# Channel statistics of a convolution: eight 128-column sums against four 32-column strips with a folding product

## The chip, the cores and the metric

One core of a Trainium2 chip runs the whole program in one launch. The metric is the device time of that core in microseconds (us), median of the runs; lower is better.

## The reference, cut to what matters

The program is one inference step of a one-layer hybrid encoder on 320 tokens (256 prompt, 64 sample) with 1024 channels: input LayerNorm, one combined projection, a retention branch, a convolution branch, a gated merge of the two, and then a mixture of 32 experts. The change touches the LayerNorm inside the convolution branch and the gate that follows it:

```
c = lax.conv_general_dilated(u_pad, conv_w...)        # depthwise, width 31, 1024 channels
c = silu(layer_norm(c + conv_b, conv_ln_g, conv_ln_b)) # mean and variance over the 1024 channels
y_conv = c @ w_conv_out
a = (sigmoid(ga) * y_ret + sigmoid(gb) * y_conv) @ w_out
```

## The kernel before, in words

All activations between the input and the merge lie transposed: channels on the 128 partitions in KT = 8 tiles, tokens along the free axis. The convolution's result is `cT`, 128 x 8 x 350: 350 columns (CCOLS), of which 320 are tokens. Its mean over channels is therefore a sum over partitions and over 8 tiles, and TensorE makes it: `mean` (L1430 to L1439) multiplies a constant 128 x 128 matrix `meanw`, filled with 1/1024, with each tile of `cT` and accumulates the 8 products in bank 7 of PSUM, so that every partition of the bank holds the mean. The variance is made in the same way from the squares `sq` (L1445 to L1450). These products are fp32, and each shows in the trace as two MATMUL rows (two passes).

The weights of all dense products come as a stream of 45 chunks of 1 MB, in the order of the program: chunks 24 to 27 are the retention output (RET0), 28 to 31 the second gate (GB0 to GB0+3), 32 the embedding projection (PROJ0), 33 to 36 the convolution output (CONV0). For each chunk i, ScalarE makes a high part (`hi(i)`, L466) and VectorE the rest (`lo(i)`, L710), and TensorE forms three fp32r products of 320 columns for each of 8 x 2 weight tiles (`wide`, L1258 to L1268, products L1254 to L1256), 48 products in all. There are two buffers for the parts: `hi(i)` waits until TensorE has done chunk i-2, `wide(i)` waits for `lo(i)`.

The order on every engine is written out by hand. TensorE does: mean of tiles 0 to 4, chunk 28, mean of tiles 5 to 7, chunk 29, the eight products of `sq`, chunk 30, chunk 31, the projection in two column halves b = 0 and b = 1 (L1452 to L1474), chunk 33. VectorE and ScalarE each run a loop over i = 0 to 44 whose body begins with `lo(i)` or `hi(i)` and then does what is listed for that i:

- VectorE, i = 29: wait for the mean, subtract it from the 8 tiles (L1088). i = 30: the low part of the router weights and of `pT`, then wait for the variance, add EPS into `cstat` (L1096). i = 31: reciprocal (L1099), 8 products (L1101), low parts `CT_lo` (L1105). i = 32: more of these.
- ScalarE, i = 29: 8 squares (L607). i = 30: `pT_hi`. i = 31: square root of `cstat` (L589), then `silu` and high part (L599, L602) of tiles 0 and 1. i = 32: `silu` and high part of tiles 2 to 7.
- The sigmoid of a gate chunk (L595) stands in ScalarE's order by the table `SIGMOIDS_AT`: the chunks 28 and 29 one step after their number, 30 and 31 both at i = 33, behind `hi(33)` and all silus.

The projection's half b = 1 writes banks 7, 0 and 1, and waits for the sigmoid of chunk 30 to have read banks 0 and 1.

Of the kernel before, what the change touches and what calls it, by code (L numbers as in the profile page):

```python
# [9 lines left out]
TOK = SEQ + DEC_SEQ  # L10
TILES = 3
ROWS = [128, 128, 64]
KT = D_MODEL // 128
# [4 lines left out]
CCOLS = UCOLS - HIST  # L18
# [13 lines left out]
GLU0, QKV0, G0, GA0, RET0, GB0, PROJ0, CONV0, OUT0, GATE0, DENSE = 0, 8, 16, 20, 24, 28, 32, 33, 37, 41, 45  # L32
# [17 lines left out]
C_PRIO8 = C_PRIO4 + 4  # L50
C_FOLD = C_PRIO8 + 8
C_P = C_FOLD + 36
C_N = C_P + 1
NOWHERE = 4096

TAP_GROUPS = ((1, 2), (3, 4), (5, 6, 7))
# [4 lines left out]
def _constants():  # L61
    c = np.zeros((128, C_N), np.float64)
    p = np.arange(128)
    c[:, C_ID:C_ID + 128] = np.eye(128)
    c[:, C_ONES:C_ONES + 128] = 1.0 / D_MODEL
    scale = DK ** -0.5
    for h, g in enumerate(GAMMA):
        m = C_MASK + 448 * h
        for first, cols in ((0, np.arange(256)), (128, np.arange(128, 256))):
            src, dst = (first + p)[:, None], cols[None, :]  # L70
            seen = (dst >= src) | (dst // CHUNK == src // CHUNK)
            c[:, m + 2 * first:m + 2 * first + len(cols)] = np.where(seen, g ** np.abs(dst - src), 0.0) * scale
        l = np.arange(64)
        c[:64, m + 384:m + 448] = g ** np.abs(l[None, :] - l[:, None]) * scale
        c[:, C_XI + 64 * h:C_XI + 64 * (h + 1)] = g ** (l + 1.0)
        for t in range(TILES):
            last = 255 - 128 * t - p if t < 2 else np.maximum(63 - p, 0)
            c[:, C_ZETA + 4 * t + h] = g ** last * scale
    half = DK // 2
    inv = np.float32(10000.0) ** (-np.arange(half, dtype=np.float32) / np.float32(half))  # L80
    for t in range(TILES):
        pos = (128 * t + p if t < 2 else PAST_LEN + p % 64).astype(np.float32)
        ang = pos[:, None] * inv[None, :]
        c[:, C_COS + 64 * t:C_COS + 64 * (t + 1)] = np.cos(ang)
        c[:, C_SIN + 64 * t:C_SIN + 64 * (t + 1)] = np.sin(ang)
    c[:, C_IOTA:C_IOTA + 64] = np.arange(64)
    c[:, C_EOFF:C_EOFF + EXPERTS] = SLOTS * np.arange(EXPERTS)
    c[:, C_PRIO4:C_PRIO4 + 4] = 4 - np.arange(4)
    c[:, C_PRIO8:C_PRIO8 + 8] = 8 - np.arange(8)
    c[:72, C_FOLD:C_FOLD + 36] = np.concatenate([np.eye(36), np.eye(36)])  # L90
    c[:, C_P] = p
    return c.astype(np.float32)


# [25 lines left out]
def _program(nc, wstream, x, p_t, state_ret, state_conv, consts, triangle, conv_params, route_w, route_b,  # L120
             ln_in, ln1, ln2, y, ret_p, ret_s, conv_p, conv_s):
    F, R, B16 = mybir.dt.float32, mybir.dt.float32r, mybir.dt.bfloat16
# [17 lines left out]
    def area(name, size=None, skip=0):  # L140
        return Area(nc, spot[name] + skip, size if size else sizes[name] - skip)

    a = area("fixed")
    const = a.put("const", [128, C_N], F)
# [9 lines left out]
    a = area("split")  # L154
    whi = a.put("w_hi", [128, 2, CH], R)
    wlo = a.put("w_lo", [128, 2, CH], R)
    a = area("h")
    hT = [a.put("hT_hi", [128, KT, TOK], R), a.put("hT_lo", [128, KT, TOK], R)]
    uT = area("u").put("uT_sb", [128, KT, UCOLS], F)
    cT = area("c").put("cT_sb", [128, KT, CCOLS], F)  # L160
    a = area("qk")
# [3 lines left out]
    a = area("v")  # L165
# [8 lines left out]
    a = area("ret", end - spot["ret"])  # L174
# [7 lines left out]
    a = area("g")  # L182
# [7 lines left out]
    a = area("qk")  # L190
    AT = [a.put("AT_hi", [128, KT, TOK], R), a.put("AT_lo", [128, KT, TOK], R)]
    a = area("v")
    CT = [a.put("CT_hi", [128, KT, CCOLS], R), a.put("CT_lo", [128, KT, CCOLS], R)]
    sq = area("u").put("sq", [128, KT, CCOLS], F)
    a = area("h")
    mT = [a.put("m_hi", [128, KT, TOK], R), a.put("m_lo", [128, KT, TOK], R)]
    a = area("ret", end - spot["ret"])
    cstat = a.put("cstat", [128, CCOLS], F)
    at_tmp = Area(nc, spot["ret"] + 4096, 3584).put("at_tmp", [128, 2, TOK], F)

    a = area("h")
# [4 lines left out]
    a = Area(nc, spot["u"] + 2 * CH * 4, spot["v"] - spot["u"] - 2 * CH * 4)  # L206
# [5 lines left out]
    a = area("ga", end - spot["ga"])  # L212
# [5 lines left out]
    a = area("g", skip=CH * 4)  # L218
    logT = a.put("logT", [72, TOK], F)
    onehot = a.put("onehot", [128, TILES, SLOTS], B16, 2)  # L220
    a = area("fixed", 4 * (C_IOTA - C_MASK), skip=4 * C_MASK)
# [17 lines left out]
    a = Area(nc, pT_at, 7680)  # L239
# [22 lines left out]
        "affine_psum affine_T norm_ready h_rows hT_psum hraw_act hraw_dve hT_hi hT_lo ln_in_rows_in rows_scaled rows_done hT_last h1T_last gate_last hi_ready lo_ready pe_done wide_free row_free sig_ready v_ready qk_rows "  # L262
        "heads_T heads_copied kz_ready q_scaled scores masked kv_ready kv_out state_new o_ready on_ready "
        "diag_ready conv0_psum conv0_ready states_out ret_p_out out_tile route_hi route_lo "
        "onT_psum at_ready at_hi at_lo taps_done mean_ready centred squared var_ready cstd_ready conv_norm "
        "silu_ready ct_hi ct_lo m_ready m_hi_ready m_lo_ready out_evac "
        "var_in root_out h1_rows h1T_psum h1T_hi_s h1T_lo_s pT_hi_s pT_lo_s part_hi part_rest part_mid part_last "
        "logT_psum logT_ready logit_psum gexp_in gexp eexp_in eexp taken_ready rank_psum "
# [10 lines left out]
    def ss(name):  # L279
        return s[name]  # L280
# [177 lines left out]
    def _(act):  # L458
# [49 lines left out]
            go(kv_s[:], ps[:, 7, DV:2 * DV], ACT.Copy).then_inc(ss("kv_out"), 1)  # L508


        SIGMOIDS_AT = {c + 1: (c,) for c in [*range(GA0, RET0), GB0, GB0 + 1]}
        SIGMOIDS_AT[GB0 + 5] = (GB0 + 2, GB0 + 3)

        def merged_high(c):
            act.wait_ge(ss("m_ready"), c + 1)
# [186 lines left out]
    def _(dve):  # L702
# [338 lines left out]
        for i in range(DENSE):  # L1041
# [41 lines left out]
            conv(TAPS_AT.get(i, 0))  # L1083
            if i == 29:
                dve.wait_ge(ss("taps_done"), n_taps)
                dve.wait_ge(ss("mean_ready"), 1)
                for j in range(KT):
                    tt(cT[:, j, :], cT[:, j, :], ps[:, 7, 0:CCOLS], ALU.subtract).then_inc(ss("centred"), 1)  # L1088
            if i == 30:
                dve.wait_ge(ss("route_hi"), 1)  # L1090
                tt(w_route_r[:, :, 1, :], w_route[:], w_route_r[:, :, 0, :].bitcast(F), ALU.subtract).then_inc(ss("route_lo"), 1)
                dve.wait_ge(ss("pT_hi_s"), 1)
                tt(pT[1][:], pT_raw[:], pT[0][:].bitcast(F), ALU.subtract).then_inc(ss("pT_lo_s"), 1)
                dve.wait_ge(ss("var_ready"), 1)
                dve.wait_ge(ss("states_out"), 16)
                ts(cstat[:], ps[:, 7, 0:CCOLS], EPS, None, ALU.add).then_inc(ss("cstd_ready"), 1)  # L1096
            if i == 31:
                dve.wait_ge(ss("cstd_ready"), 2)
# [150 lines left out]
    def _(pe):  # L1249
# [5 lines left out]
            mm(out, wh, xl, start=False, stop=False)  # L1255
            return mm(out, wl, xh, start=False, stop=last)  # L1256

        def wide(c, par, src, cols, credit, banks=None):  # L1258

            pe.wait_ge(ss("lo_ready"), c)  # L1260
            pe.wait_ge(ss("wide_free"), credit)
            w = [q[:, par, :].rearrange("p (k c) -> p k c", k=KT) for q in (whi, wlo)]
            for t in range(2):
                out = ps[:, (2 * par if banks is None else banks) + t, 0:cols]
                for k in range(KT):
                    m = three(out, w[0][:, k, 128 * t:128 * t + 128], w[1][:, k, 128 * t:128 * t + 128],
                              src[0][:, k, :], src[1][:, k, :], k == 0, k == KT - 1)
            m.then_inc(ss("pe_done"), 1)  # L1268

        def last_tile(out_bank, x2, w, start, stop):  # L1270
# [161 lines left out]
        def mean(tiles):  # L1432
            for j in tiles:
                if j:
                    pe.wait_ge(ss("taps_done"), CONV_W * max(g[-1] for g in TAP_GROUPS if g[0] <= j))
                else:
                    pe.wait_ge(ss("conv0_ready"), 1)
                m = mm(ps[:, 7, 0:CCOLS], meanw, cT[:, j, :], start=j == 0, stop=j == KT - 1)
            return m  # L1439

        pe.wait_ge(ss("at_ready"), KT)
        mean(range(5))
        wide(GB0, 0, hT, TOK, 21)
        mean(range(5, KT)).then_inc(ss("mean_ready"), 1)
        wide(GB0 + 1, 1, hT, TOK, 22)  # L1445
        pe.wait_ge(ss("centred"), KT)
        for j in range(KT):
            pe.wait_ge(ss("squared"), j + 1)
            m = mm(ps[:, 7, 0:CCOLS], meanw, sq[:, j, :], start=j == 0, stop=j == KT - 1)
        m.then_inc(ss("var_ready"), 1)  # L1450
        wide(GB0 + 2, 0, hT, TOK, 23)
        wide(GB0 + 3, 1, hT, TOK, 24)  # L1452

        pe.wait_ge(ss("lo_ready"), PROJ0)
# [292 lines left out]
```

## Time and profile before

| what | value |
|---|---|
| median of 3 runs | 933.31 us (933.19 to 935.58) |
| the profiled execution | 933.24 us |
| its span in the profile | 931.1 us |
| TensorE busy | 867.5 us, 93% of the span |
| VectorE, ScalarE busy | 423.9 us, 260.0 us |
| chain that ended last | PE 56%, DMA 32%, DVE 6%, ACT 3% |

The profiled execution took 2.1 us more than its span, which begins with the first instruction and ends with the last. PE is TensorE (PEld its weight loads), DVE is VectorE, ACT is ScalarE, SP is the engine that issues the weight transfers. The statistics and the second gate lie between 267 and 316 us of the span. The experts' weights, 1 MB at a time, are streamed from 370 us to near 900 us.

### The profile page before, as it was taken

The page shows a single profiled execution, that of the slowest core. Times are in us where ns is not written, and L with a number is a line of the kernel's source. Part 1 is how long each engine was busy: PE and PEld are TensorE (multiplying, and loading weights), DVE is VectorE, ACT ScalarE, POOL GpSimd, SP SyncE. Part 2 cuts the span into 40 slices and gives each one's busy share as a digit, 9 for nine tenths or more (in the row PEclk, how much of TensorE's full clock was granted, in tenths as well). Part 3 has the DMA queues.
Part 4 walks back from the last instruction along what each step waited for, and adds up shares of the span by engine and source line. Part 5 has one row for each costly group of instructions (what it writes and reads, how often), then busy time and mean ns, then how long its engine had stood idle before and what let it go on. Part 6 is the DMA issues. An engine that isn't in the chain of part 4 may idle for free.

```text
span 931.1 us, 16368 instructions
## 1 busy us (share of the span) xinstructions
PE 867.5 (93%) x6542; PEld 558.8 (60%) x6542; DVE 423.9 (46%) x784; ACT 260.0 (28%) x356; POOL 49.4 (5%) x89
## 2 busy tenths in 40 slices
PE   8999999999999899899999999989888989898975
PEld 5997777789999796676444444434343434444431
DVE  6589799988967458965221111101010101011036
ACT  5451224444317723344112111111111212111110
POOL 1200000000000000000000000000000000000000
PEclk9999999999999999999999999999999999999997
DMA  8842233233433435945999999999999999999961
GB/s 318 274 164 72 99 146 118 91 113 114 150 139 133 147 136 180 372 152 223 414 420 421 422 422 421 422 422 421 423 422 423 422 422 421 422 422 422 421 253 56
DMA packets 40516, 266.66 MB, mean 286 GB/s; under 512 B 6214, under 2 KB 6486, under 8 KB 9632
## 3 DMA queue, kind: packets, MB, share of 16 engines
q1 hardware_dynamic: 36064, 255.30, 68.2%
q0 software_dynamic: 4416, 10.86, 3.6%
q8 instruction: 25, 0.41, 0.2%
q14 instruction: 11, 0.09, 0.0%
HBM read 258.38 MB, written 13.09 MB: 292 GB/s over the span
## 4 chain that ended last, share of the span: by engine, by line
PE 56%; DMA 32%; DVE 6%; ACT 3%; issue 2%; SPq 1%; DVEq 0%; ACTq 0%
DMA raw_x<-wstream 30%; PE ps L1557 12%; PE ps L1254 7%; PE ps L1255 6%; PE ps L1256 6%; PE ps L1568 3%; PE ps L1528 3%; PE ps L1291 2%; PE ps L1273 2%; PE ps L1292 2%; PE ps L1293 2%; PE ps L1351 2%; ACT w_hi L466 1%; DVE w_lo L710 1%; PE ps L1301 1%
## 5 line engine op out<-in xcount | busy, mean ns | idle before, releaser
L1557 PE MATMUL ps<-raw_x,xs 128*64 128x512 f32 x1024 | 233.6, 596 | 35.2 <-DMA raw_x<-wstream 34.0
L1557 PEld LDWEIGHTS ps<-raw_x,xs 128*64 128x64 f32 x1024 | 79.9, 136 | 160.3 <-issue 158.3
L710 DVE TENSOR_TENSOR w_lo<-raw_dense,w_hi 128x2048 fp32r<-128x2048 f32 x44 | 101.9, 2315 | 36.0 <-ACT w_hi L466 35.9
L1568 PE MATMUL ps<-raw_x,actT 128*64 128x512 f32 x512 | 117.8, 597 | 0.0
L1180 DVE COPY actT<-ps 128x256 f32<-128x256 f32 x32 | 13.6, 424 | 222.6 <-PE ps L1575 222.6
L466 ACT ACTIVATE w_hi<-raw_dense 128x2048 fp32r<-128x2048 f32 x44 | 84.0, 1908 | 97.7 <-PE ps L1273 62.7
L842 DVE SCALAR_TENSOR_TENSOR cT_sb<-uT_sb,conv_par,cT_sb 128x350 f32<-128x350 f32 x210 | 106.8, 574 | 0.6
L1254 PE MATMUL ps<-hT_hi,w_hi 128*128 128x320 f32 x304 | 95.5, 314 | 0.2 <-issue 0.2
L1256 PE MATMUL ps<-hT_hi,w_lo 128*128 128x320 f32 x304 | 93.9, 309 | 0.0
L1255 PE MATMUL ps<-hT_lo,w_hi 128*128 128x320 f32 x304 | 93.9, 309 | 0.0
L1186 DVE SCALAR_TENSOR_TENSOR act_rows<-gate_silu,slot_weight,ps 64x512 f32<-64x512 f32 x32 | 23.7, 740 | 139.3 <-ACT gate_silu L649 139.3
L1528 PEld LDWEIGHTS ps<-onehot,h1b 128*128 128x128 bf16 x2304 | 69.0, 98 | 25.4 <-issue 25.4
L649 ACT ACTIVATE gate_silu<-ps 64x512 f32<-64x512 f32 x32 | 19.0, 593 | 233.2 <-PE ps L1557 233.2
L1528 PE MATMUL ps<-onehot,h1b 128*128 128x64 bf16 x2304 | 72.7, 193 | 0.0
L1568 PEld LDWEIGHTS ps<-raw_x,actT 128*64 128x64 f32 x512 | 40.3, 137 | 50.3 <-issue 49.6
L1254 PEld LDWEIGHTS ps<-hT_hi,w_hi 128*128 128x128 f32 x304 | 57.1, 188 | 2.3 <-issue 1.4
L1255 PEld LDWEIGHTS ps<-hT_lo,w_hi 128*128 128x128 f32 x304 | 57.1, 188 | 0.3
L1256 PEld LDWEIGHTS ps<-hT_hi,w_lo 128*128 128x128 f32 x304 | 57.1, 188 | 0.0
L654 ACT ACTIVATE y_sb<-ps 64x512 f32<-64x512 f32 x30 | 17.7, 590 | 96.0 <-PE ps L1568 96.0
L645 ACT ACTIVATE xs<-ps 128x512 f32<-128x512 f32 x32 | 19.1, 597 | 53.6 <-PE ps L1528 53.6
L440 POOL DMA_INDIRECT y_rows<-y_sb,y_to_now x30 | 27.1, 902 | 25.7 <-POOL y_to_now L437 25.7
L437 POOL COPY y_to_now<-y_to 64x1 uint32 x30 | 5.3, 178 | 432.7 <-ACT y_sb L655 432.7
(288 smaller groups left out, 1063.6 us busy)
## 6 DMA issues: line engine op xcount, KB each, us to landing
raw_x<-wstream SPq DMA_DIRECT2D x192, 1024.0 KB, 24.2
raw_dense<-wstream SPq DMA_DIRECT2D x45, 1024.0 KB, 4.8
y_rows<-rows_sb POOLq DMA_DIRECT2D x10, 256.0 KB, 8.7
ln_gb<-ln POOLq DMA_DIRECT2D x2, 1024.0 KB, 5.0
y_gathered<-y_rows SPq DMA_DIRECT2D x4, 512.0 KB, 5.8
const<-consts SPq DMA_DIRECT2D x1, 1294.5 KB, 12.2
rows_sb<-x SPq DMA_DIRECT2D x2, 512.0 KB, 3.7
ln_gb<-ln_in POOLq DMA_DIRECT2D x1, 1024.0 KB, 4.8
```

The lines of the kernel that those rows point to most:

```text
L440: pool.indirect_dma_start(out=y_rows, out_offset=bass.IndirectOffsetOnAxis(ap=y_to_now[:], axis=0), in_=ysb[:], in_offset=None, bounds_che ...
L466: go(whi[:, i % 2, :], raw_d[:, i % RAW_D, :], ACT.Copy).then_inc(ss("hi_ready"), 1)
L645: go(xs[:], ps[:, 7, :].rearrange("p (k s) -> p k s", k=KT), ACT.Copy).then_inc(ss("x_ready"), 1)
L710: tt(wlo[:, i % 2, :], raw_d[:, i % RAW_D, :], whi[:, i % 2, :].bitcast(F), ALU.subtract).then_inc(ss("lo_ready"), 1)
L842: i = stt(out=cT[:, j, :], in0=src, scalar=w, in1=cT[:, j, :], op0=ALU.mult, op1=ALU.add)
L1186: stt(out=act_rows[:], in0=gsil[:], scalar=slot_w[:], in1=ps[0:64, 1, :], op0=ALU.mult, op1=ALU.mult).then_inc(ss("act_ready"), 1)
L1254: mm(out, wh, xh, start=first, stop=False)
L1255: mm(out, wh, xl, start=False, stop=False)
L1256: return mm(out, wl, xh, start=False, stop=last)
L1528: m = mm(ps[:, 7, SLOTS * k:SLOTS * k + SLOTS], h1b[:, part, t, 128 * k:128 * k + 128], onehot[:, t, :], start=part == 0 and t == 0, stop= ...
L1557: m = mm(ps[rows_at, 1, :], xs[:, 4 * half + k, :], w[i][:, k, :], start=half == 0 and k == 0, stop=half == 1 and k == 3)
L1568: m = mm(ps[64 * b:64 * b + 64, 4, :], aT[:, 2 * half + k, :], w[:, k, FF * b:FF * b + FF], start=half == 0 and k == 0, stop=half == 1 and ...
```

## The change

TensorE's sums over channels use 32 output columns each, in four strips of the array: tile j goes to strip j mod 4, so that strip c (partitions 32c to 32c+31 of bank 7) holds the sum of tiles c and c+4, divided by 32. VectorE copies bank 7 to a new tile `cparts`, and one 128 x 128 product with the old `meanw` adds the four strips. That product stands inside the next chunk, behind the first 9 of its 48 products. VectorE's wait for `states_out` (a transfer out of the place where `cparts` now lies) moves from i = 30 to i = 29. In ScalarE's order the sigmoid of chunk 30 moves from i = 33 to i = 31. The table of constants grows by 32 columns.

```diff
-C_N = C_P + 1
+C_PART = C_P + 1
+C_N = C_PART + 32
...
+    c[:, C_PART:C_N] = 1.0 / 32
...
     cstat = a.put("cstat", [128, CCOLS], F)
+    cparts = a.put("cparts", [128, CCOLS], F)
...
-        SIGMOIDS_AT = {c + 1: (c,) for c in [*range(GA0, RET0), GB0, GB0 + 1]}
-        SIGMOIDS_AT[GB0 + 5] = (GB0 + 2, GB0 + 3)
+        SIGMOIDS_AT = {c + 1: (c,) for c in [*range(GA0, RET0), GB0, GB0 + 1, GB0 + 2]}
+        SIGMOIDS_AT[GB0 + 5] = (GB0 + 3,)
...
             if i == 29:
                 dve.wait_ge(ss("taps_done"), n_taps)
+                dve.wait_ge(ss("mean_parts"), 1)
+                dve.wait_ge(ss("states_out"), 16)
+                V.tensor_copy(cparts[:], ps[:, 7, 0:CCOLS]).then_inc(ss("mean_parts_in"), 1)
                 dve.wait_ge(ss("mean_ready"), 1)
...
             if i == 30:
+                dve.wait_ge(ss("var_parts"), 1)
+                V.tensor_copy(cparts[:], ps[:, 7, 0:CCOLS]).then_inc(ss("var_parts_in"), 1)
                 dve.wait_ge(ss("route_hi"), 1)
...
-                dve.wait_ge(ss("states_out"), 16)
                 ts(cstat[:], ps[:, 7, 0:CCOLS], EPS, None, ALU.add).then_inc(ss("cstd_ready"), 1)
...
-        def wide(c, par, src, cols, credit, banks=None):
+        def wide(c, par, src, cols, credit, banks=None, within=None):
...
+                    if within and t == 0 and k == 2:
+                        within()
...
-                m = mm(ps[:, 7, 0:CCOLS], meanw, cT[:, j, :], start=j == 0, stop=j == KT - 1)
+                m = part_sums(j, cT)
             return m
+
+        def part_sums(j, src):
+
+            c = j % 4
+            return mm(ps[32 * c:32 * c + 32, 7, 0:CCOLS], const[:, C_PART:C_N], src[:, j, :], start=j < 4, stop=j >= 4)
+
+        def whole_sums(parts_in, signal):
+
+            pe.wait_ge(ss(parts_in), 1)
+            mm(ps[:, 7, 0:CCOLS], meanw, cparts[:], start=True, stop=True).then_inc(ss(signal), 1)
...
-        mean(range(5, KT)).then_inc(ss("mean_ready"), 1)
-        wide(GB0 + 1, 1, hT, TOK, 22)
+        mean(range(5, KT)).then_inc(ss("mean_parts"), 1)
+        wide(GB0 + 1, 1, hT, TOK, 22, within=lambda: whole_sums("mean_parts_in", "mean_ready"))
...
-            m = mm(ps[:, 7, 0:CCOLS], meanw, sq[:, j, :], start=j == 0, stop=j == KT - 1)
-        m.then_inc(ss("var_ready"), 1)
-        wide(GB0 + 2, 0, hT, TOK, 23)
+            m = part_sums(j, sq)
+        m.then_inc(ss("var_parts"), 1)
+        wide(GB0 + 2, 0, hT, TOK, 23, within=lambda: whole_sums("var_parts_in", "var_ready"))
         wide(GB0 + 3, 1, hT, TOK, 24)
```

The order on TensorE around the start of chunk 29 (`hT` by the gate's weights), of the kernel before. A row is a product, `x3` a run of equal ones, and the brackets name the semaphores that it waits on:

```order
L1438 MATMUL ps<-cT_sb,const 128x350 [waits taps_done] x3
L1254 MATMUL ps<-hT_hi,w_hi 128x320 [waits wide_free,lo_ready]
L1255 MATMUL ps<-hT_lo,w_hi 128x320
L1256 MATMUL ps<-hT_hi,w_lo 128x320
L1254 MATMUL ps<-hT_hi,w_hi 128x320
L1255 MATMUL ps<-hT_lo,w_hi 128x320
```

And of the changed kernel, in the same place (its lines are numbered otherwise: L1453 is `part_sums`, L1261 to L1263 are the three products of `wide`, L1458 is `whole_sums`):

```order
L1453 MATMUL ps<-cT_sb,const 32x350 [waits taps_done] x3
L1261 MATMUL ps<-hT_hi,w_hi 128x320 [waits wide_free,lo_ready]
L1262 MATMUL ps<-hT_lo,w_hi 128x320
L1263 MATMUL ps<-hT_hi,w_lo 128x320
L1261 MATMUL ps<-hT_hi,w_hi 128x320
L1262 MATMUL ps<-hT_lo,w_hi 128x320
L1263 MATMUL ps<-hT_hi,w_lo 128x320
L1261 MATMUL ps<-hT_hi,w_hi 128x320
L1262 MATMUL ps<-hT_lo,w_hi 128x320
L1263 MATMUL ps<-hT_hi,w_lo 128x320
L1458 MATMUL ps<-cparts,const 128x350 [waits mean_parts_in]
L1261 MATMUL ps<-hT_hi,w_hi 128x320
```

The three sums have 32 output rows where they had 128, and the folding product stands as the tenth of chunk 29, with a wait of its own. The same happens at the start of chunk 30.

The order on ScalarE from `hi(31)` on, of the kernel before:

```order
L466 ACTIVATE w_hi<-raw_dense 128x2048 [waits pe_done,raw_dense_in3]
L589 ACT_TABLE_LOAD
L589 ACTIVATE cstat<-cstat 128x350 [waits cstd_ready]
L599 ACT_TABLE_LOAD
L599 ACTIVATE cT_sb<-cT_sb,conv_par 128x350 [waits conv_norm]
L602 ACTIVATE CT_hi<-cT_sb 128x350 [waits silu_ready]
```

And of the changed kernel (L592 is the square root, L598 the sigmoid, L602 the silu, L605 the high part):

```order
L469 ACTIVATE w_hi<-raw_dense 128x2048 [waits pe_done,raw_dense_in3]
L592 ACT_TABLE_LOAD
L592 ACTIVATE cstat<-cstat 128x350 [waits cstd_ready]
L598 ACT_TABLE_LOAD [waits wide_free]
L598 ACTIVATE sB<-ps 128x640 [waits pe_done]
L602 ACT_TABLE_LOAD
L602 ACTIVATE cT_sb<-cT_sb,conv_par 128x350 [waits conv_norm]
L605 ACTIVATE CT_hi<-cT_sb 128x350 [waits silu_ready]
```

The sigmoid, its wait for TensorE (`pe_done`) and a table load stand ahead of the first silu; a second table load returns to the silu.

## Rows read from the trace of the kernel before

**Rows 1.** The page: span, TensorE's busy time, the chain that ended last.

```profile
span 931.1 us, 16368 instructions
PE 867.5 (93%) x6542; PEld 558.8 (60%) x6542; DVE 423.9 (46%) x784; ACT 260.0 (28%) x356; POOL 49.4 (5%) x89
PE 56%; DMA 32%; DVE 6%; ACT 3%; issue 2%; SPq 1%; DVEq 0%; ACTq 0%
```

**Rows 2.** Timeline of PE, 267 to 316 us: start, duration, line, [idle before].

```profile
267.63 3.11 PE L1438 MATMUL ps<-cT_sb,const 128*128 128x350 f32 x10
270.72 0.31 PE L1255 MATMUL ps<-hT_lo,w_hi 128*128 128x320 f32 x1
...
277.61 1.93 PE L1438 MATMUL ps<-cT_sb,const 128*128 128x350 f32 x6
...
279.52 0.31 PE L1255 MATMUL ps<-hT_lo,w_hi 128*128 128x320 f32 x1
...
286.41 4.88 PE L1449 MATMUL ps<-sq,const 128*128 128x350 f32 x16
...
291.27 0.31 PE L1255 MATMUL ps<-hT_lo,w_hi 128*128 128x320 f32 x1
...
311.57 0.47 PE L1466 MATMUL ps<-w_hi,pT_hi 128*128 128x512 f32 x1 [2.44 <-ACT sB L595]
```

**Rows 3.** Timeline of PE where two 64-column strips work, and their end.

```profile
308.04 0.44 PE L1273 MATMUL ps<-raw_dense,pT_raw 128*64 128x256 f32 x2
...
314.18 0.39 PE L1468 MATMUL ps<-w_hi,pT_lo 128*128 128x512 f32 x1
314.50 1.08 PE L1273 MATMUL ps<-raw_dense,pT_raw 128*64 128x256 f32 x8
...
315.77 0.32 PE L1255 MATMUL ps<-CT_lo,w_hi 128*128 128x350 f32 x1
```

**Rows 4.** Timeline of DVE, 279 to 312 us.

```profile
279.65 3.52 DVE L1088 TENSOR_TENSOR cT_sb<-cT_sb,ps 128x350 f32<-128x350 f32 x8 [7.32 <-PE ps L1438]
285.87 2.29 DVE L710 TENSOR_TENSOR w_lo<-raw_dense,w_hi 128x2048 fp32r<-128x2048 f32 x1 [2.70 <-ACT w_hi L466]
...
291.32 0.52 DVE L1096 TENSOR_SCALAR cstat<-ps 128x350 f32<-128x350 f32 x1 [2.06 <-PE ps L1449]
...
296.33 3.56 DVE L1101 TENSOR_TENSOR cT_sb<-cT_sb,cstat 128x350 f32<-128x350 f32 x8
...
301.04 2.29 DVE L710 TENSOR_TENSOR w_lo<-raw_dense,w_hi 128x2048 fp32r<-128x2048 f32 x1 [0.29 <-ACT w_hi L466]
...
309.44 2.29 DVE L710 TENSOR_TENSOR w_lo<-raw_dense,w_hi 128x2048 fp32r<-128x2048 f32 x1 [1.28 <-ACT w_hi L466]
```

**Rows 5.** Timeline of ACT, 280 to 319 us.

```profile
283.94 1.90 ACT L466 ACTIVATE w_hi<-raw_dense 128x2048 fp32r<-128x2048 f32 x1
286.61 0.70 ACT L595 ACTIVATE sB<-ps 128x640 f32<-128x640 f32 x1 [0.77 <-PE ps L1256]
287.21 0.73 ACT L612 ACTIVATE pT_hi<-pT_raw 128x640 fp32r<-128x640 f32 x1
...
296.89 0.68 ACT L599 ACTIVATE cT_sb<-cT_sb,conv_par 128x350 f32<-128x350 f32 x1 [3.21 <-DVE cT_sb L1101]
...
309.42 1.28 ACT L595 ACT_TABLE_LOAD   x1
310.72 1.50 ACT L595 ACTIVATE sB<-ps 128x640 f32<-128x640 f32 x2
...
315.63 1.09 ACT L617 ACTIVATE base_rows<-ps 128x512 f32<-128x512 f32 x2 [1.78 <-PE ps L1273]
...
317.28 1.90 ACT L466 ACTIVATE w_hi<-raw_dense 128x2048 fp32r<-128x2048 f32 x1
```

**Rows 6.** Stretch 500 to 900 us: us; busy PE, PEld, DVE, ACT, POOL; PEclk, DMA share, GB/s.

```profile
500.00:900.00 400.00, 365.93 (x3394) 171.11 (x3394) 45.92 (x135) 62.91 (x106) 28.01 (x52) 1.00 1.00 417
```

**Rows 7.** Waits of the SP queue, 320 to 931 us.

```profile
SPq L348 <- PE ps L1557: 195.8, 61, 6.0
```

More of the change, by code:

```diff
@@ L264, in _program @@
         "diag_ready conv0_psum conv0_ready states_out ret_p_out out_tile route_hi route_lo "
-        "onT_psum at_ready at_hi at_lo taps_done mean_ready centred squared var_ready cstd_ready conv_norm "
+        "onT_psum at_ready at_hi at_lo taps_done mean_parts mean_parts_in mean_ready centred squared var_parts var_parts_in var_ready cstd_ready conv_norm "
         "silu_ready ct_hi ct_lo m_ready m_hi_ready m_lo_ready out_evac "
```

## The prediction

> **What bounds the kernel now.** Three views, in this order. First the page [rows 1]: TensorE is busy 93% of 931.1 us and holds 56% of the chain that ended last, transfers 32%. That says which engine, not which stage. Then TensorE's timeline through the touched stretch [rows 2]: it works without a gap from the sums at 267.63 to the projection's first half, then stands 2.44 us for a sigmoid of ScalarE. Last the timelines of VectorE and ScalarE in the same stretch [rows 4, 5], since they decide where a shortened TensorE will have to wait. The reader should see that up to 291 us TensorE is the bound, and from the normalisation on it is ScalarE: eight silus with their high parts, `hi(32)` and `hi(33)` fill it from 296.89 to 309.4 us, and the sigmoid that TensorE waits for stands behind them.
>
> To compare starts I use the second product of a chunk less one spacing of 0.147 us (48 products took 7.04 us from 270.57 to 277.61), since the first overlaps the product ahead of it in the records [rows 2]. Chunks 28, 29 and 30 began at 270.57, 279.37 and 291.12 us, chunk 33 at 315.77 less 0.16, which is 315.61 us [rows 2, 3]. What the change does to this last number is the whole question: later stages wait on it and on what follows it alone.
>
> **The strips.** One fp32 product of 350 columns is two passes of 0.294 us (10 took 2.94 from 267.63 to 270.57) [rows 2]. In four strips four of them should run at once. The trace has no 32-column strip; the nearest row has two of 64 columns. There the first two passes, in different strips, last 0.44 us together, no longer than one pass with its recorded tail (3.11 - 9 x 0.294 = 0.46, of 350 columns) [rows 2, 3]; and 8 passes of 256 columns are over 1.11 us after 314.50, where 8 in a row would need 8 x 0.215 = 1.72 us (0.294 x 256/350 = 0.215 for one) [rows 3]. So strips overlap, pass by pass. That row also has the price of going to strips and back: from the end of the 512-column product (314.18 + 0.23) to 315.61 are 1.20 us for 4 x 0.215 = 0.86 us of work, so 0.34 us a visit.
>
> Bounds for a strip group: full overlap (0.587 us for up to four products), overlap of two (0.587 us a pair), none (0.587 us each). I take full overlap, by the row nearest to it, where every strip used did overlap. With 0.34 us a visit:
> - tiles 0 to 4 (four, then one): 1.17 + 0.34 = 1.51 us where 2.94 stood; chunk 28 begins at 269.14 and ends at 276.18;
> - tiles 5 to 7: 0.59 + 0.34 = 0.93 where 1.76 stood; chunk 29 begins at 277.11;
> - squares: 1.17 + 0.34 = 1.51 where 4.71 stood.
>
> The Trainium skill (TensorE: Matmul & The Clock Gate, on packing small matmuls) gives 2.38 times for three column strips of 512 columns, so less than three. By it the groups would be a quarter longer, some 0.3 us in sum up to the mean, and the gain below would be 2.6. No row here has three strips.
>
> **The folding product and the mean.** VectorE is idle before the mean (7.32 us) [rows 4], so its copy costs nothing but latency: it starts some 0.28 us after the last pass (279.37 to 279.65 now), and takes about 0.5 us like L1096 [rows 4]. The fold is the tenth product of chunk 29, at 277.11 + 9 x 0.147 = 278.43; the copy is done at about 277.6, so TensorE does not wait. The fold adds 0.587 us to the chunk and ends at 279.02. The subtraction starts at 279.30, against 279.65: only 0.35 us earlier, although 2.26 us of TensorE's time are gone, because the fold came in between. `hi(30)` follows the squares at a fixed distance (279.65 to 283.94), so it starts at 283.6, and `lo(30)` ends at 287.7 (285.87 + 2.2 less 0.35) [rows 4, 5]. That `lo(30)` was hidden: it ended at 288.1, with TensorE still at the squares until 291.12. Now chunk 29 ends at 277.11 + 7.04 + 0.59 = 284.74 and the strips of the squares at 286.25. **TensorE is early and stands 1.6 us for `lo(30)`**; chunk 30 begins at about 287.95. Of the 4.9 us that TensorE saves up to here (291.12 - 286.25, one fold counted), 3.2 remain.
>
> Chunk 30 with its fold ends at 295.58. The copy for the variance stands behind `lo(30)`, at about 287.7 to 288.2, and the fold is due at 289.3, so no wait. `cstat` comes at 290.1 in place of 291.32, the normalisation's first product at 295.1 in place of 296.33 [rows 4].
>
> **The sigmoid.** ScalarE now waits for chunk 30 before its first silu. TensorE to sigmoid 0.2 us, sigmoid 0.6, table load 1.28 [rows 5]: the first silu is at 297.7, against 296.89, **0.8 us later** although its input is 1.2 us earlier. The load ahead of the sigmoid is covered, between the root at about 290.7 and 295.6. Queued behind are all silus, `hi(32)` and `hi(33)`, each 0.8 late. So `lo(32)` ends at 304.1 (now 303.3) [rows 4], and TensorE, done with chunk 31 at 302.6, stands 1.5 us for it. The projection's two halves then run through, since banks 0 and 1 are free: 2 x 4.04 us (311.57 to 315.61) gives 312.3 [rows 2, 3]. `lo(33)` starts at 310.24 and ends at 312.5 [rows 4]; the last sigmoid ends at 312.2. Chunk 33 begins at about 312.7, against 315.61. **Gain 2.9 us.** `hi(34)` stands behind the copies of both halves, 1.65 us each (315.63 to 317.28) [rows 5]: from 312.2 that gives 315.5, `lo(34)` ends at 319.7 (1.9 + 0.1 + 2.2 later), and chunk 33 lasts at least 48 x 0.16 us, to 320.4, so the next chunk does not wait.
>
> **Edits with one cost.** The `states_out` wait is met long before. 16 KB more of constants are below 0.1 us at any rate in the rows (417 GB/s) [rows 6].
>
> **To the end.** From 500 to 900 us the weight stream runs at a DMA share of 1.00 [rows 6]. It could swallow the gain if it had a start of its own, but SP's refills wait for TensorE [rows 7], and the first ones come behind the merge. All of it moves together. So 933.24 - 2.9 = 930.3 us; the profiled execution is 0.07 us off the median, so the same holds against that. Its own range: visits at no cost would give 0.7 us more (929.6), the skill's factor aside a visit of twice the price 0.7 less (931.0).
>
> **Rivals.**
> - *Only two strips at once.* For: the only rows of overlap have two. Against: nothing in them shows a limit. The sums up to the fold take 1.17 us more (one more group each time); the squares stay hidden under `lo(30)`. Gain 1.7, 931.5 us. Chance 0.15.
> - *No overlap of 32-column strips: slower.* Then the products cost as much as before, and come with 3 visits and 2 folds. Chunk 28 begins at 270.9, 29 at 280.04, the squares take 287.67 to 292.7, chunk 30 ends at 300.3. The sigmoid's wait in front of the silus turns this into loss: chunk 33 follows chunk 30's end by 312.7 - 295.58 = 17.1 us, so the change loses as soon as chunk 30 ends after 298.5. Here chunk 33 begins at 317.4: 1.8 us lost, 935.1 us. Against it stand rows 3. Chance 0.05.
> - *The gain is made here and not kept.* A wait further on (for example `lo(34)`, 0.7 us from being late, or a refill) takes 1 to 3 us back: 931.3 to 933.2, say 932.5 us. For: a DMA share of 1.00. Against: its issues wait for TensorE. Chance 0.20.
> - *More than forecast.* ScalarE's chain has room I did not count, and TensorE's own arrival or less sets chunk 33: 929.4 us. Chance 0.10.
> - Forecast: 0.50.
>
> **How the numbers follow.** About 0.3% (2.8 us) is what a measurement of this kernel can tell from no change; that bound is 930.5 us against the median, inside my forecast's own range. About three quarters of the forecast's 0.50 lie below it, all of the larger gain: faster 0.48. The two-strip case, the lost gain, the loss of 1.8 us (0.2%) and the rest of the forecast are within it: same 0.47. Slower by more than 0.3% needs no overlap and something more: 0.05. The range is 929.0 to 933.2: it leaves out the slower cases, and half of a tail on either side.
>
> **What the profile after would show.** Strips: the eight squares end 1.2 to 1.3 us after they begin, plus a visit; each fold's two rows stand inside a chunk with no idle time ahead. TensorE waits about 1.6 us for `w_lo` ahead of chunk 30 and 1.5 us ahead of the projection, and no longer for the sigmoid. First silu near 297.7, chunk 33 near 312.7. A wait ahead of a fold, a squares group of 2.4 us or more, or a first silu after 298.5 would make it wrong; so would chunk 33 at 312.7 with a time above 932.

## The result, and the profile after

| | before | changed |
|---|---|---|
| median, first measurement | 933.9 us (933.19 to 935.58) | 929.03 us (928.24 to 930.25) |
| profiled execution, span | 933.24, 931.1 us | 930.25, 928.2 us |
| TensorE busy | 867.5 us | 863.3 us |

The ratio is 0.9946, with a 95% interval of 0.9934 to 0.9959: the change is faster, by about 5 us, where 3.0 were forecast. The profile agrees with the forecast, the medians do not: the two spans are 2.9 us apart. The ratio, applied to the 933.31 us shown ahead of the prediction, gives 928.3 us. One more execution of the changed kernel, in its third measurement below, took 3013.49 us and is in no median here; nothing on record says why.

The page of the changed kernel, the lines that answer to [rows 1]:

```profile
span 928.2 us, 16378 instructions
PE 863.3 (93%) x6546; PEld 554.0 (60%) x6546; DVE 425.0 (46%) x786; ACT 261.1 (28%) x357; POOL 49.4 (5%) x89
PE 55%; DMA 32%; DVE 6%; ACT 4%; issue 2%; SPq 1%; ACTq 0%; DVEq 0%
```

Its TensorE timeline, which answers to [rows 2]:

```profile
267.55 1.36 PE L1453 MATMUL ps<-cT_sb,const 128*32 128x350 f32 x10
...
269.09 0.31 PE L1262 MATMUL ps<-hT_lo,w_hi 128*128 128x320 f32 x1
...
276.08 0.79 PE L1453 MATMUL ps<-cT_sb,const 128*32 128x350 f32 x6
...
278.22 0.75 PE L1458 MATMUL ps<-cparts,const 128*128 128x350 f32 x2
...
284.61 1.39 PE L1453 MATMUL ps<-sq,const 128*32 128x350 f32 x16
...
287.58 0.41 PE L1261 MATMUL ps<-hT_hi,w_hi 128*128 128x320 f32 x1 [1.58 <-DVE w_lo L713]
...
304.03 0.50 PE L1485 MATMUL ps<-w_hi,pT_hi 128*128 128x512 f32 x1 [1.52 <-DVE w_lo L713]
...
312.48 0.40 PE L1261 MATMUL ps<-CT_hi,w_hi 128*128 128x350 f32 x1 [0.42 <-DVE w_lo L713]
312.72 0.33 PE L1262 MATMUL ps<-CT_lo,w_hi 128*128 128x350 f32 x1
```

The 16 passes over the squares last 1.39 us where 16 lasted 4.88. The folds stand inside their chunks with no idle time ahead. TensorE now waits 1.58 us for `lo(30)` and 1.52 us for `lo(32)`, and no longer for the sigmoid. Ahead of chunk 33 it waits 0.42 us for `lo(33)`.

VectorE and ScalarE of the changed kernel, which answer to [rows 4, 5]:

```profile
276.98 0.52 DVE L1091 COPY cparts<-ps 128x350 f32<-128x350 f32 x1 [4.82 <-issue]
279.01 3.52 DVE L1094 TENSOR_TENSOR cT_sb<-cT_sb,ps 128x350 f32<-128x350 f32 x8 [1.51 <-PE ps L1458]
285.23 2.29 DVE L713 TENSOR_TENSOR w_lo<-raw_dense,w_hi 128x2048 fp32r<-128x2048 f32 x1 [2.70 <-ACT w_hi L469]
...
294.80 3.56 DVE L1108 TENSOR_TENSOR cT_sb<-cT_sb,cstat 128x350 f32<-128x350 f32 x8
...
310.09 2.29 DVE L713 TENSOR_TENSOR w_lo<-raw_dense,w_hi 128x2048 fp32r<-128x2048 f32 x1 [1.28 <-ACT w_hi L469]
```

```profile
295.51 0.70 ACT L598 ACTIVATE sB<-ps 128x640 f32<-128x640 f32 x1 [3.36 <-PE ps L1263]
296.24 1.28 ACT L602 ACT_TABLE_LOAD   x1
297.53 0.68 ACT L602 ACTIVATE cT_sb<-cT_sb,conv_par 128x350 f32<-128x350 f32 x1
```

ScalarE stands 3.36 us for chunk 30, loads the silu's table behind the sigmoid, and starts the silus 0.64 us later than before (297.53 for 296.89) although their input is 1.53 us earlier (294.80 for 296.33).

**A common origin.** The start of `hi(28)`, ahead of which nothing was changed, differs by up to 1.3 us between the profiles. So all stages below are compared from the start of `hi(28)`, the last ScalarE row ahead of the changed part, to the second product of chunk 33. ScalarE's timeline near 268 us, of the kernel before and of the changed one:

```profile
267.88 1.91 ACT L466 ACTIVATE w_hi<-raw_dense 128x2048 fp32r<-128x2048 f32 x1 [5.33 <-PE ps L1256]
```

```profile
267.71 1.91 ACT L469 ACTIVATE w_hi<-raw_dense 128x2048 fp32r<-128x2048 f32 x1 [5.33 <-PE ps L1263]
```

Before it is 315.77 [rows 3] - 267.88 = 47.89 us, in the changed kernel 312.72 - 267.71 = 45.01. **The stage gains 2.88 us**; the sum said 2.9. Two further profiles of the changed kernel give 44.99 and 45.00. From there to the end of the span are 615.4 us before and 615.5, 615.2 and 614.8 us in the three profiles of the changed kernel; over all 14 profiles of this document they are 613.5 to 616.5 us, so single executions scatter by more than the gain there.

### The profile page after: what moved, and what is told of

It is laid out like the page before. It is cut to its first block, busy times and chain, and to the rows that moved or that the text cites. A ratio compares the mean times of both kernels' runs of the same rounds, so it can differ in the third digit from the quotient of the medians.

```text
span 928.2 us, 16378 instructions
## 1 busy us (share of the span) xinstructions
PE 863.3 (93%) x6546; PEld 554.0 (60%) x6546; DVE 425.0 (46%) x786; ACT 261.1 (28%) x357; POOL 49.4 (5%) x89
## 4 chain that ended last, share of the span: by engine, by line
PE 55%; DMA 32%; DVE 6%; ACT 4%; issue 2%; SPq 1%; ACTq 0%; DVEq 0%
DMA raw_x<-wstream 31%; PE ps L1576 12%; PE ps L1261 7%; PE ps L1263 6%; PE ps L1262 6%; PE ps L1587 3%; PE ps L1547 3%; PE ps L1300 2%; PE ps L1282 2%; PE ps L1301 2%; PE ps L1302 2%; PE ps L1360 2%; ACT w_hi L469 1%; DVE w_lo L713 1%; PE ps L1310 1%
## 5 line engine op out<-in xcount | busy, mean ns | idle before, releaser
L1261 PE MATMUL ps<-hT_hi,w_hi 128*128 128x320 f32 x304 | 95.6, 314 | 1.8 <-DVE w_lo L713 1.6
L1263 PE MATMUL ps<-hT_hi,w_lo 128*128 128x320 f32 x304 | 93.9, 309 | 0.0
L1261 PEld LDWEIGHTS ps<-hT_hi,w_hi 128*128 128x128 f32 x304 | 57.1, 188 | 5.6 <-DVE w_lo L713 2.5
L1263 PEld LDWEIGHTS ps<-hT_hi,w_lo 128*128 128x128 f32 x304 | 57.1, 188 | 0.0
```

The source lines that it names most:

```text
L1261: mm(out, wh, xh, start=first, stop=False)
```

## The experiments

The open question was where 2 us more came from. The theories:

- A: the stage's gain reaches the end one to one and the rest is scatter.
- B: the change gives 2 us more somewhere behind the stage.
- C and D: one of the two parts, the sigmoid's move (C) or the strips (D), gives nearly all.
- E, added when the first four runs were seen: TensorE's 2.44 us wait in the kernel before [rows 2] often lowers its clock, and the change ends this.
- F: the clock has no part.

"Stage" is the distance just defined, from one profile each; "gain" is against 47.89 us. The kernel before, run beside all of them, gave a median of 934.60 us in 69 executions; 933.31 was a low draw of three. Every execution reports the mean of TensorE's granted clock over its whole length; the last column says in how many it was 0.991 or less. For the kernel before they were 44 of 69, in the first measurement of the changed kernel 0 of 4.

| kernel | stage, us | stage gain | median, us | ratio to before (95%) | clock 0.991 or less |
|---|---|---|---|---|---|
| changed, again | 44.99 | 2.90 | 930.64 | 0.9955 (0.9940 to 0.9971) | 2 of 6 |
| changed, third time | 45.00 | 2.89 | 929.96 | 0.9952 (0.9937 to 0.9967) | 1 of 5 |
| constants only | 47.90 | 0.0 | 935.26 | 1.0012 (0.9998 to 1.0026) | 7 of 12 |
| sigmoid only | 47.67 | 0.22 | 932.93 | 0.9985 (0.9974 to 0.9995) | 1 of 12 |
| strips only | 47.93 | 0.0 | 933.71 | 0.9991 (0.9982 to 1.0001) | 10 of 11 |
| before, wait filled | 47.85 | 0.0 | 932.76 | 0.9984 (0.9975 to 0.9993) | 2 of 12 |
| strips only, wait filled | 46.45 | 1.44 | 932.45 | 0.9977 (0.9967 to 0.9987) | 5 of 12 |
| two strips | 46.22 | 1.67 | 931.23 | 0.9959 (0.9944 to 0.9975) | 1 of 4 |
| one strip | 49.83 | -1.94 | 935.42 | 1.0007 (0.9998 to 1.0017) | 2 of 10 |
| fold after 3 products | 44.43 | 3.46 | 929.35 | 0.9943 (0.9930 to 0.9956) | 0 of 6 |
| high parts split | 42.89 | 5.00 | 927.54 | 0.9928 (0.9915 to 0.9942) | 1 of 6 |
| all three | 42.41 | 5.48 | 926.63 | 0.9916 (0.9901 to 0.9930) | 0 of 5 |

### The changed kernel once more, and the constants alone

> The changed kernel once more, to tell what the change gives in total. In the profiled executions chunk 33 began 3.05 us earlier (312.56 for 315.61) and the span was 2.9 us shorter, while the medians lay 4.9 us apart. Theory A (the gain is made before chunk 33 and reaches the end one to one; the rest is scatter of single executions in the expert stage): chunk 33 at 312.6, ratio 0.9967 or 3.1 us. Theory B (the change gives about 2 us more somewhere behind chunk 33 in most executions): ratio about 0.995 again, 4.5 to 5 us, chunk 33 still at 312.6.

Stage 44.99 us, median 930.64 us, ratio 0.9955: 4.05 us gained between the medians, 2.9 in the stage. The surplus is there again, but theory A's 0.9967 lies inside this interval (0.9940 to 0.9971). It is the first measurement that excludes it (0.9934 to 0.9959). Theory B is not seen in the profiles: behind the stage they show no gain (615.5, 615.2 and 614.8 us against 615.4).

```diff
-C_N = C_P + 1
+C_PART = C_P + 1
+C_N = C_PART + 32
...
+    c[:, C_PART:C_N] = 1.0 / 32
```

> The kernel before with nothing but the 32 more columns of constants, which no instruction reads; all tiles behind the constants move by 128 bytes per partition. Theory A: no difference, ratio 1.000, chunk 33 at 315.6. Theory B in the form that the moved layout gives the surplus: about 2 us faster, ratio 0.998, with chunk 33 at 315.6 all the same.

Ratio 1.0012 (0.9998 to 1.0026), stage 47.90. The moved layout gives nothing that can be told from noise.

### One part at a time

```diff
-        SIGMOIDS_AT = {c + 1: (c,) for c in [*range(GA0, RET0), GB0, GB0 + 1]}
-        SIGMOIDS_AT[GB0 + 5] = (GB0 + 2, GB0 + 3)
+        SIGMOIDS_AT = {c + 1: (c,) for c in [*range(GA0, RET0), GB0, GB0 + 1, GB0 + 2]}
+        SIGMOIDS_AT[GB0 + 5] = (GB0 + 3,)
```

> The kernel before with only the sigmoid of chunk 30 moved to i = 31. Theory A, worked as in the prediction: chunk 30 ends at 298.16 as before, the sigmoid comes at 298.3, after a table load the first silu at 300.3 (now 296.9), so lo(32) ends at 306.7, the projection runs 306.8 to 314.9 without a stop, lo(33) ends at 315.1 and chunk 33 begins at 315.2: 0.4 us gained, ratio 0.9996. Theory C (the sigmoid's move is what makes most of the gain, since it ends the 2.44 us wait of TensorE): 2 us or more, chunk 33 at 313.2.

Stage gain 0.22 us, where theory A had 0.4 and theory C 2 or more. But the median fell by 1.8 us, which nothing in the stage explains. This was the first sign that the removed wait counts for more than its length.

> The changed kernel with the sigmoid of chunk 30 back at i = 33. Theory A: the normalisation starts at 294.8 as in the changed kernel (1.53 us earlier than before), the silus follow it at once, the first at 295.4, hi(33) and the sigmoid end 1.5 us earlier, the projection's second half starts at 310.04 and chunk 33 at 314.1: 1.5 us gained, ratio 0.9984. Theory D (the strips alone give the whole gain and the sigmoid's move is neutral): 3 us, chunk 33 at 312.6. By theory A the two parts give 0.4 and 1.5 alone and 3.05 together.

This is the change with the table of sigmoids put back. 1.5 us were expected in the stage, none came; the median is 1.0 us lower, at the edge of the noise. ScalarE did as forecast; TensorE did not. Its timeline behind the wait for the sigmoid, and the stretches (us, then busy PE, PEld, DVE, ACT, POOL, granted clock, DMA share, GB/s):

```profile
310.06 0.76 PE L1485 MATMUL ps<-w_hi,pT_hi 128*128 128x512 f32 x1 [3.76 <-ACT sB L598]
310.63 0.63 PE L1486 MATMUL ps<-w_lo,pT_hi 128*128 128x512 f32 x1
311.05 0.63 PE L1487 MATMUL ps<-w_hi,pT_lo 128*128 128x512 f32 x1
...
313.16 0.39 PE L1486 MATMUL ps<-w_lo,pT_hi 128*128 128x512 f32 x1
313.39 0.40 PE L1487 MATMUL ps<-w_hi,pT_lo 128*128 128x512 f32 x1
```

```profile
306.00:310.00 4.00, 0.31 (x4) 0.00 (x0) 2.59 (x2) 3.89 (x4) 0.55 (x1) 0.96 0.65 215
310.00:312.00 2.00, 1.94 (x5) 1.58 (x6) 0.23 (x1) 1.97 (x5) 0.00 (x0) 0.50 0.65 266
```

After 3.76 us of standing still TensorE is granted half its clock (1.2 of 2.4 GHz), and its products come every 0.43 us in place of 0.23. Seven of them ran so, 7 x 0.20 = 1.4 us: the whole gain. The strips had made TensorE earlier at a place where it then waits longer, and the longer wait cost what the strips gave.

### Filling the waits

Of the 69 executions of the kernel before, the 44 with a mean clock of 0.991 or less have a median of 934.98 us, the other 25 one of 933.80. Of 15 executions of the changed kernel 3 have 0.991 (931.3 us), 12 more (929.7 us). The profile on which the prediction rests doesn't show this cost: its clock stayed full through the wait and behind it, as its stretches from 301 to 325 us say (granted clock 1.00, third number from the end):

```profile
301.00:312.00 11.00, 8.56 (x52) 7.18 (x51) 7.55 (x8) 10.69 (x17) 0.55 (x1) 1.00 0.58 231
312.00:325.00 13.00, 13.00 (x79) 11.72 (x78) 3.62 (x4) 6.73 (x11) 0.00 (x0) 1.00 0.32 103
```

The next edit fills the wait. `keep_warm(n)` issues n products of two constants, whose result nobody reads:

```diff
                 pe.wait_ge(ss("cstd_ready"), 1)
+                keep_warm(5, bank=7)
                 pe.wait_ge(ss("wide_free"), 2 + 23)
```

> The kernel before with 5 products of two constants into the unused bank 7 (2.15 us by 0.43 us each) in TensorE's 2.44 us wait ahead of the projection's second half; the work of the program is the same. So far the before kernel's executions show a mean granted clock of 0.991 or less in 18 of 29 (median of the 10 at 0.991: 934.87 us) and 0.993 or more in 11 (933.01 us for the 7 at 0.993), the changed kernel's 0.993 in 6 of 10. Theory E (in most executions the 2.44 us wait halves TensorE's clock for a while; the changed kernel has no such wait, and that is its surplus of about 1.5 us over the 3.05 us of its profile): chunk 33 stays at 315.6, but nearly all executions have 0.993 and the median falls to about 933.0 to 933.4, ratio 0.9985. Theory F (the clock falls elsewhere, or the spread has nothing to do with that wait): ratio 1.000.

TensorE's timeline in the place of the 2.44 us wait; the ten passes fill it, and the next product starts 0.03 us behind them:

```profile
309.57 2.42 PE L1316 MATMUL ps<-const 128*128 128x256 f32 x10
312.02 0.50 PE L1467 MATMUL ps<-w_hi,pT_hi 128*128 128x512 f32 x1
```

Stage 47.85, unchanged. Median 932.76 beside 934.45: ratio 0.9984 (0.9975 to 0.9993), against 0.9985 expected; theory F's 1.000 is excluded. Ten of 12 executions are above 0.991. **Five products that compute nothing gain 1.7 us (0.7 to 2.3)**, so that much of the kernel before was the price of leaving TensorE idle for 2.44 us.

The mean clock says the same over all kernels. Where TensorE stands idle for the sigmoid at the projection (before, constants only, strips only), 61 of 92 executions have 0.991 or less. Where that wait is gone or filled (all others), 15 of 82 have. And each of these others gains more in its median than in its stage, by 0.6 to 2.5 us.

What the numbers don't do is turn the clock into the 1.7 us. Among the 29 executions of before that ran beside this one, the 10 above 0.991 have a median of 934.25 us, only 0.45 below the rest. The 10 such executions of the filled kernel have 932.42. So the gain is there between executions of equal mean clock as well, and how it divides is open.

> The kernel with strips but the old place of the sigmoid, plus 8 such products in TensorE's 3.76 us wait there. Its profile without them had a granted clock of 0.50 from 310.0 to 312.8 us, right behind that wait, and chunk 33 at 315.51 in place of the 314.1 worked out. Theory E: with the products the clock stays full, chunk 33 at 314.1, median about 931.9 (1.5 us below before's executions at full clock, 933.2 less, and 1.8 below strips_only), ratio 0.997. Theory F: as strips_only, chunk 33 at 315.5, ratio 0.999.

With 8 such products in the same place of the strips-only kernel the stage gains 1.44 us where it gained none, as expected. The median, 932.45, is 0.5 us above the value expected, and 5 of 12 executions still have a mean clock of 0.991. Its own profile, at 0.991, has no fall at the projection but one much later (the first line). So has the profile of before with the wait filled, whose mean is 0.993 all the same (the second and third line):

```profile
396.00:399.00 3.00, 3.00 (x13) 2.15 (x10) 2.54 (x15) 1.93 (x3) 0.00 (x0) 0.50 0.03 5
```

```profile
396.00:399.00 3.00, 2.84 (x22) 2.46 (x22) 2.31 (x10) 2.10 (x3) 0.00 (x0) 0.82 0.50 208
399.00:402.00 3.00, 3.00 (x10) 2.08 (x8) 2.58 (x15) 0.77 (x3) 0.00 (x0) 0.61 0.42 115
```

There TensorE is granted half its clock near 396 us, in the routing stage, which is the same in all these kernels. This fall costs nothing up to the experts: from chunk 33 to their first product (L1557 of before) are 116.71 us with the wait of before filled and 116.68 in the profile of before, which has no fall there. So it does not explain the 0.5 us. The first profile, of strips only with the wait filled, lies at the long end of the scatter behind the stage, 616.5 us. The clock falls near the end too, in every profile, and not equally long: from 900 to 920 us the granted clock is 0.83 before and 0.91 with constants only. The mean clock of one execution therefore doesn't say where the clock fell. That it fell at the projection in executions of before is inferred from the counts above and from the profile of strips only, not seen in a profile of before.

### How many strips

```diff
-C_N = C_PART + 32
+C_N = C_PART + 64
...
-    c[:, C_PART:C_N] = 1.0 / 32
+    c[:, C_PART:C_N] = 1.0 / 64
...
-            c = j % 4
-            return mm(ps[32 * c:32 * c + 32, 7, 0:CCOLS], const[:, C_PART:C_N], src[:, j, :], start=j < 4, stop=j >= 4)
+            c = j % 2
+            return mm(ps[64 * c:64 * c + 64, 7, 0:CCOLS], const[:, C_PART:C_N], src[:, j, :], start=j < 2, stop=j >= 6)
```

> The changed kernel with two strips of 64 columns for four of 32, all else the same. By the chain of the prediction the five and the three products take one more group each, 0.59 us, up to the fold of the mean, so everything from there is 1.17 us later: chunk 30 begins at 288.85, chunk 33 at 313.75. The squares take 1.17 us more but end at 288.3, still ahead of lo(30). Gain against before 1.9 us in the profile, ratio about 0.9965 with the clock's part. Rival (the squares' time is on the path as well): chunk 33 at 314.9.

Stage gain 1.67 us where four strips give 2.88, so 1.21 us later; 1.17 was expected. The squares took 2.57 us for 1.39 and were still hidden: they took it out of the wait for `lo(30)`, which is left with 0.39 of 1.58 us.

```diff
-            c = j % 4
-            return mm(ps[32 * c:32 * c + 32, 7, 0:CCOLS], const[:, C_PART:C_N], src[:, j, :], start=j < 4, stop=j >= 4)
+            return mm(ps[0:32, 7, 0:CCOLS], const[:, C_PART:C_N], src[:, j, :], start=j == 0, stop=j == KT - 1)
...
+                link(V.memset(cparts[:], 0.0))
...
-                V.tensor_copy(cparts[:], ps[:, 7, 0:CCOLS]).then_inc(ss("mean_parts_in"), 1)
+                V.tensor_copy(cparts[0:32, :], ps[0:32, 7, 0:CCOLS]).then_inc(ss("mean_parts_in"), 1)
...
-                V.tensor_copy(cparts[:], ps[:, 7, 0:CCOLS]).then_inc(ss("var_parts_in"), 1)
+                V.tensor_copy(cparts[0:32, :], ps[0:32, 7, 0:CCOLS]).then_inc(ss("var_parts_in"), 1)
```

> The changed kernel with all eight products into strip 0, one after the other, VectorE zeroing the rest of cparts while it is idle: the slower rival of the prediction made real. By its chain chunk 29 begins at 279.9, chunk 30 at 292.6 and ends at 300.2, and chunk 33 begins 17.0 us behind that, at 317.3: 1.7 us later than before, ratio 1.001 to 1.002. If instead the wait of ScalarE for chunk 30 were not what orders the rest, chunk 33 would come by TensorE's own work only, 1.2 us for the folds and 0.9 for the visits less the 2.44 us wait: at about 315.3, ratio 0.999.

TensorE's timeline with two strips and with one, the squares, and with one strip also the end of the projection's wait:

```profile
287.14 2.57 PE L1453 MATMUL ps<-sq,const 128*64 128x350 f32 x16
290.10 0.41 PE L1261 MATMUL ps<-hT_hi,w_hi 128*128 128x320 f32 x1 [0.39 <-DVE w_lo L713]
```

```profile
288.11 4.90 PE L1453 MATMUL ps<-sq,const 128*32 128x350 f32 x16
...
309.39 0.50 PE L1485 MATMUL ps<-w_hi,pT_hi 128*128 128x512 f32 x1 [1.52 <-DVE w_lo L713]
```

The slower rival, made real: 1.94 us lost in the stage, 1.8 forecast. A product of 32 columns alone costs what one of 128 does (4.90 against 4.88 us), and the sigmoid in front of the silus turns TensorE's lateness into ScalarE's. Between the medians only 1.0 us is lost, and the interval (0.9998 to 1.0017) still holds no change: this kernel too has no wait for the sigmoid at the projection, and 8 of 10 executions are above 0.991.

### Looking for a faster version

```diff
-                    if within and t == 0 and k == 2:
+                    if within and t == 0 and k == 0:
```

> The changed kernel with the folding product behind the third product of its chunk (k == 0) in place of the ninth. VectorE's copy for the mean is done about 0.6 us after chunk 29 begins, so the fold can start 0.67 us earlier at the most. Theory A (the place of the mean's fold sets the squares, hi(30), lo(30) and all behind): chunk 33 0.6 to 0.7 us earlier than in the changed kernel, taken from each run's own hi(28). Rival (the fold is not on the path, since TensorE waits before chunk 30 and the projection anyway): no change, chunk 33 stays.

The edit moves both folds. The stage gains 0.58 us, 0.6 to 0.7 expected, and chunk 30 already starts 0.57 us earlier from `hi(28)`, ahead of the variance's fold: so it is the mean's fold that is on the path. TensorE's wait for `lo(30)` shrinks from 1.58 to 0.69 us.

```diff
-    CT_PARTS = (range(2), range(2, KT), ())
+    CT_PARTS = ((), range(KT), ())
...
-                    act.wait_ge(ss("silu_ready"), j + 1)
-                    go(CT[0][:, j, :], cT[:, j, :], ACT.Copy).then_inc(ss("ct_hi"), 1)
+                    if j % 2:
+                        act.wait_ge(ss("silu_ready"), j + 1)
+                        go(CT[0][:, j, :], cT[:, j, :], ACT.Copy).then_inc(ss("ct_hi"), 1)
...
-                    dve.wait_ge(ss("ct_hi"), j + 1)
+                    if j % 2:
+                        dve.wait_ge(ss("ct_hi"), j // 2 + 1)
+                    else:
+                        dve.wait_ge(ss("silu_ready"), j + 1)
+                        link(V.tensor_copy(CT[0][:, j, :], cT[:, j, :]))
```

> The changed kernel with hi(32) and lo(32) ahead of all silus, and the high parts of tiles 0, 2, 4, 6 made by VectorE in place of ScalarE. If ScalarE's row of silus and high parts is what sets chunk 33 (the prediction's chain: hi(33) ends at 310.05, lo(33) 2.3 us later), four high parts less (0.42 us each) bring hi(33) to end at about 308.4 and chunk 33 to 310.8: 1.7 us earlier, 0.3 us behind TensorE's own arrival at 310.5. If TensorE's projection sets it, chunk 33 comes by what lo(32) gives, 1.5 us earlier, with no wait for w_lo ahead of it. If VectorE becomes the bound with its four more operations, less than 1 us.

2.12 us of the stage, more than either number expected (1.7 and 1.5). The edit does two things, `hi(32)` ahead of the silus and half of the high parts on VectorE; what each gives was not measured. TensorE no longer waits ahead of the projection or of chunk 33: the row for chunk 33 has no idle time before it.

```profile
310.40 0.40 PE L1266 MATMUL ps<-CT_hi,w_hi 128*128 128x350 f32 x1
310.64 0.33 PE L1267 MATMUL ps<-CT_lo,w_hi 128*128 128x350 f32 x1
```

> Both edits of fold_early and highs_split, and two products of constants (0.86 us) into the free bank 4 in TensorE's wait ahead of chunk 30. If the terms add, chunk 33 is 2.3 us earlier than in the changed kernel, and the median 2.3 us below it, near 927.5 to 928 us; ratio against before 0.993.

Stage gain 5.48 us, 2.60 more than the changed kernel (2.3 expected); median 926.63 us against 929.96 of the changed kernel beside it, ratio to before 0.9916 (0.9901 to 0.9930). It is the fastest kernel of this document. TensorE has no idle time left between 262 and 318 us, with the two idle products counted as work.

> The changed kernel a third time, beside the three above on the same chip. By theory E its total gain is 2.9 us in the stage and about 1.5 us by the clock: median about 930.1 us, 4.4 us under before, ratio 0.9953, and the mean granted clock at 0.992 or more in two of three executions. By theory F (no part of the clock) 2.9 us, ratio 0.9969.

929.96 us and 0.9952, with 5 executions of the changed kernel in the comparison, 4 of them above 0.991. Theory E gave 930.1 and 0.9953, theory F 0.9969, just outside the interval (0.9937 to 0.9967).

## Why the prediction was right or wrong

**Right, within 0.3 us each, in the one profiled execution** (the starts that follow are as the profile has them; its origin lies 0.17 us earlier):
- The strips. Full overlap of four, with a price for the visit: 0.34 us taken from two 64-column strips. The chain of starts (chunk 28 at 269.14, 29 at 277.11, 30 at 287.95) came at 268.94, 276.90 and 287.68 (second product less 0.147). The first visit took 1.17 + 0.31 us. The rule of the Trainium skill (TensorE: Matmul & The Clock Gate, on packing small matmuls) of 2.38 times for three strips would have made it longer: the five and three products took 1.48 and 0.92 us, below the 1.51 and 0.93 forecast without it. Here, with fp32 passes of 350 columns, three and four strips run at the pace of one, so the page's figure, for 512 columns, does not hold for them.
- The fold's place: ready in time, no wait, the subtraction 0.47 us earlier by the common origin (279.65 to 279.01, less 0.17; 0.35 forecast), so that most of TensorE's saving ends in a wait for `lo(30)`, 1.58 us (1.6 forecast).
- The sigmoid: first silu at 297.53 (297.7), the wait for `lo(32)` 1.52 us (1.5), chunk 33 at 312.56 (312.7).
- The rivals on strips: two strips 1.67 us in the stage (1.7), one strip -1.94 (-1.8).
- The stage's 2.9 us reach the end: 2.9 us between the two spans. The rival that they are lost further on has nothing for it: 615.4 us behind the stage before, 614.8 to 615.5 in the changed kernel.

**Wrong: the size of the whole, by the last step.** The failed step is the sentence that ends the sum: "So 933.24 - 2.9 = 930.3 us; the profiled execution is 0.07 us off the median, so the same holds against that." The term it lacks is what TensorE's 2.44 us wait for the sigmoid costs beyond its length. The prediction priced the wait at its length, and in the profile it read it cost no more. Filling it with idle products, and nothing else, lowered the median of before by 1.7 us (0.7 to 2.3; before, wait filled: 934.45 to 932.76). The change takes that wait away by moving the sigmoid, and gets both: 2.9 + 1.7 = 4.6 us, against 4.65 between the medians over all executions (934.60 and 929.95). With an interval that wide, so close an agreement is in part luck. By what means the wait costs this is shown in part only: TensorE's clock, by the counts of the mean clock and by the profile of strips only, where 3.76 us of waiting were followed by 1.4 us lost at half the clock. How much of the 1.7 us that is stays open.

As a time of the changed kernel 930.3 was 0.35 us off its median; it was the kernel before that was typically 1.3 us slower than the median shown (934.60 and 933.31). One of the three runs shown was at 935.58, so the three did not say what was typical, and "0.07 us off the median" leaned on them. The chance of 0.48 for faster by over 0.3% was too low for the same reason: the bound lay inside the forecast only because this term was missing.

**Also missed:** that the two parts need each other. Alone the strips gave nothing in the stage and the sigmoid 0.22 us, together 2.88. With the wait filled the strips alone gave 1.44. The prediction treats the two as one sum and says of neither what it gives alone.

## What to carry to other kernels

A wait on TensorE can have two prices, its length and something beyond it, here 1.7 us for a wait of 2.44, and the second need not show in the one execution that was profiled. So look at several executions' times and mean clocks before taking one profile as typical, and try filling such a wait with idle products where a bank is free. When a stage on the bounding engine is shortened, follow the chain to what is late next: the strips shortened TensorE's work by 4.9 us up to chunk 30, gave 1.44 us alone with the wait filled, and 2.9 us when the sigmoid was moved with them. Where the output of a sum over partitions needs few columns, strips gave here, for fp32 products of 350 columns, nearly a factor equal to their number (16 passes in 4.88, 2.57 and 1.39 us for one product at a time, two strips and four), and a visit of 0.3 us comes on top.

## What the runs showed of the hardware that was not expected

- A TensorE wait of 3.76 us was followed by 3 us at half the clock (granted 0.50, products 0.43 us apart for 0.23). A wait of 2.44 us was not, in the one profile of before, and filling it gained 1.7 us in the median.
- Executions of one kernel differ in TensorE's mean clock, and idle time at one place shifts the share: 0.991 or less in 61 of 92 executions with the wait for the sigmoid, in 15 of 82 without. A fall near 396 us in the routing stage cost nothing up to the experts (116.71 against 116.68 us from chunk 33).
- In four strips the first passes of the first four squares begin within 0.02 us (284.61 to 284.63 us), and the 16 passes of eight products take 1.39 us in all; a lone 32-column strip takes 4.90 us for the same 16.
- `hi(28)`, with the same work ahead of it, begins between 267.7 and 269.0 us in different profiles. Differences below 1 us between two profiles have to be taken from an origin next to the changed part.
